# Weight tiles multiplied term by term, and a triangular inverse whose blocks VectorE turns

## The reference

```python
h = _rmsnorm(s, norm_pre_mix) * (1 + sc_a) + sh_a       # latent and context
proj = h @ w_in                                         # k, v, q, gates, z, hyena
# group A, 8 heads of 128: conv, silu, l2norm of q and k, then per chunk, both directions
a_strict   = where(strict, beta * (k k^T) * exp(diff), 0)
lower_unit = a_strict + eye
sol = triangular_solve(lower_unit, [v*beta, k*beta*exp(gcum)])
s_next = s * exp(g_last) + (k * exp(g_last - g))^T @ (u - w @ s)      # scan over the chunks
# group B: order-2 Hyena long convolution by FFT
out = concat([o, y]) @ w_out
s = s + g_a * _rmsnorm(out, norm_post_mix)
h = _rmsnorm(s, norm_pre_ffn) * (1 + sc_f) + sh_f
ff = (silu(h @ w_gate) * (h @ w_up)) @ w_down           # D_FF = 5632
s = s + g_f * _rmsnorm(ff, norm_post_ffn)
```

## Time and profile before

| | us |
|---|---|
| median of 3 runs | 1667.03 |
| the three runs | 1659.72, 1667.03, 1667.48 |
| the profiled execution | 1659.05 |
| its span | 1657.4 |
| PE busy | 1608.8 (97%), 10074 matmuls |
| DVE busy | 1148.5 (69%) |
| ACT busy | 769.1 (46%) |
| mean granted TensorE clock | 0.993 |

### The profile page before, as it was taken

How to read it: one execution, slowest core, us unless ns; L and a number is a source line. 1 busy time by engine, 2 the same in 40 slices (tenths; PEclk the granted TensorE clock), 3 DMA queues, 4 the chain that set the end, 5 groups by cost and what they waited for, 6 DMA issues and landing times.

```text
span 1657.4 us, 26938 instructions
## 1 busy us (share of the span) xinstructions
PE 1608.8 (97%) x10074; PEld 1398.9 (84%) x10074; DVE 1148.5 (69%) x1699; ACT 769.1 (46%) x1285; POOL 117.1 (7%) x214
## 2 busy tenths in 40 slices
PE   6998999999999999999998999999999999999997
PEld 2356999999998998999998888888888888888886
DVE  4726889899898997776777555555555555655665
ACT  3436465564646556433346444444444444343331
POOL 1001010110101010000110000000000000111110
PEclk9998999999999999999999999999999999999999
DMA  9996354453544545324993444554455446877872
GB/s 367 414 356 237 121 166 153 134 179 121 172 138 132 171 133 185 102 102 154 342 330 140 152 182 175 200 202 175 180 202 198 172 187 242 283 247 253 281 250 93
DMA packets 83067, 332.59 MB, mean 201 GB/s; under 512 B 8073, under 2 KB 24538, under 8 KB 56668
## 3 DMA queue, kind: packets, MB, share of 16 engines
q1 hardware_dynamic: 63168, 262.44, 43.1%
q0 software_dynamic: 19408, 67.77, 12.3%
q10 hardware_dynamic: 396, 1.10, 0.2%
HBM read 327.09 MB, written 4.19 MB: 200 GB/s over the span
## 4 chain that ended last, share of the span: by engine, by line
PE 82%; DMA 8%; DVE 5%; ACT 2%; DVEq 1%; issue 1%; SPq 0%; ACTq 0%
PE g L490 10%; PE o L490 10%; PE o L483 7%; PE o L484 7%; PE o L485 7%; PE g L491 5%; PE o L491 5%; DMA w_mod_tile_o<-in_w_mod_t 4%; DMA w_mod_raw<-in_w_mod_t 4%; PE g L566 2%; PE o L497 2%; PE g L497 2%; PE o L499 2%; PE g L499 2%; PE g L498 2%; PE g L577 2%
## 5 line engine op out<-in xcount | busy, mean ns | idle before, releaser
L464 DVE TENSOR_TENSOR w_lo<-w_raw,w_hi 128x2048 fp32r<-128x2048 f32 x202 | 462.4, 2289 | 201.8 <-ACT w_hi L459 201.4
L459 ACT CAST w_hi<-w_raw 128x2048 fp32r<-128x2048 f32 x203 | 388.0, 1911 | 219.3 <-PE o L499 73.9
L483 PE MATMUL o<-h_hi,w_hi 128*128 128x256 f32 (+1 forms) x880 | 291.6, 331 | 2.3 <-ACT hy_x L1232 1.3
L485 PE MATMUL o<-h_hi,w_lo 128*128 128x256 f32 (+1 forms) x880 | 275.3, 313 | 0.0
L484 PE MATMUL o<-h_lo,w_hi 128*128 128x256 f32 (+1 forms) x880 | 275.1, 313 | 0.0
L490 PE MATMUL g<-h_hi_lo,w_hi 128*128 128x512 f32 x704 | 245.0, 394 | 0.0
L490 PE MATMUL o<-h_hi_lo,w_hi 128*128 128x512 f32 x688 | 240.5, 394 | 2.0 <-DVE h_hi_lo L2036 2.0
L491 PE MATMUL g<-h_hi_lo,w_lo 128*128 128x256 f32 x704 | 195.0, 277 | 0.0
L491 PE MATMUL o<-h_hi_lo,w_lo 128*128 128x256 f32 x688 | 190.6, 277 | 0.0
L483 PEld LDWEIGHTS o<-h_hi,w_hi 128*128 128x128 f32 x880 | 168.0, 191 | 13.6 <-issue 6.9
L485 PEld LDWEIGHTS o<-h_hi,w_lo 128*128 128x128 f32 x880 | 167.4, 190 | 10.4
(11 more groups left out here) (393 smaller groups left out, 2820.1 us busy)
## 6 DMA issues: line engine op xcount, KB each, us to landing
w_raw<-in_w_ff_t SPq DMA_DIRECT2D x88, 1024.0 KB, 6.1
w_raw<-in_w_heads_t SPq DMA_DIRECT2D x56, 1024.0 KB, 4.9
w_mod_raw<-in_w_mod_t SPq DMA_DIRECT2D x32, 1024.0 KB, 11.1
w_raw<-in_w_down_t SPq DMA_DIRECT2D x32, 1024.0 KB, 6.8
w_mod_piece_h<-in_w_mod_t POOLq DMA_DIRECT2D x112, 256.0 KB, 3.6
w_raw<-in_w_out_t SPq DMA_DIRECT2D x16, 1024.0 KB, 8.4
w_mod_tile_o<-in_w_mod_t POOLq DMA_DIRECT2D x16, 1024.0 KB, 9.8
w_mod_piece_d<-in_w_mod_t POOLq DMA_DIRECT2D x64, 256.0 KB, 5.9
```

The lines of the kernel that those rows point to most:

```text
L459: e.copy(whi[p.split[j]][:], raw[p.raw[j]][:]).then_inc(hi_ready, 1)
L464: e.tensor_tensor(wlo[p.split[j]][:], raw[p.raw[j]][:], whi[p.split[j]][:].bitcast(F32), ALU.subtract).then_inc(lo_ready, 1)
L483: e.matmul(o, a, xh, start=first, stop=False)
L485: return e.matmul(o, b, xh, start=False, stop=last)
```

## The change

1. The three matmuls of a block no longer stand together. `mm_term` runs a tile's 16 upper x upper matmuls, then the 16 upper x lower, then the 16 lower x upper. PE waits for the upper part before the first, and for the lower part only before the last third. The FFN does its 16 matmuls of 512 columns and then its 16 of 256. Not changed are the k and v tiles of head 0, the first two tiles of the output projection, the first two of the FFN, and the down projection.
2. For the levels 2 to 5 the steps `X{n}` (ACT) and `DN{n}` (PE) are gone. DVE turns X straight from PSUM by 32x32 blocks, drains, and masks the result in place. Level 6, with blocks of 64, stays as it was.
3. The steps `v0` to `v3` move from DVE to ACT. `v0` runs at the end of the head before, the others at the end of `vs0` to `vs2`. Three drains ahead of `w{n}` on DVE go, and `w{n}` waits for ACT's `v{n}`. PE's `z0` waits for `Z` of DVE explicitly.
4. In the lists some steps change places: `D3` goes ahead of the attention masks, `D4` ahead of the convolution `cv(2)`, `D5` ahead of a piece, and a weight piece each ahead of `UT2` and `UT5`.

```diff
+        def mm_term(e, o, p, i, j, xh, xl, r0, r1, n=KT_N):
+            s = p.split[j]
+            for r in range(r0, r1):
+                term, k = r // n, r % n
+                if r == 0:
+                    upper_ready(e, p, i, j)
+                elif r == 2 * n:
+                    lower_ready(e, p, i, j)
+                last = e.matmul(o, (wlo if term == 2 else whi)[s][:, k * P:(k + 1) * P], (xl if term == 1 else xh)(k),
+                                start=(r == 0), stop=(r == 3 * n - 1))
+            return last
...
-            inv("UT1"); scan("z3"); pr(15); scan("o3"); inv("DN2"); inv("Y2"); pr(16); inv("UT2"); pr(17); pr(18); pr(19)
-            inv("DN3"); inv("Y3"); pr(20); pr(21); inv("UT3"); pr(22); pr(23); inv("DN4"); inv("Y4"); pr(24); pr(25)
+            inv("UT1"); scan("z3"); pr(15); scan("o3"); inv("Y2"); pr(16); pr(17); inv("UT2"); pr(18); pr(19)
+            inv("Y3"); pr(20); pr(21); inv("UT3"); pr(22); pr(23); inv("Y4"); pr(24); pr(25)
...
             def ff_tiles(p, i, m0, j0=0):
                 for j in range(j0, 4):
-                    tile_ready(pe, p, i, j)
                     b = (O[0], O[1], G[2], G[3])[j]
+                    pe.wait_ge(hi_ready, st.tile(p, i, j) + 1)
                     pe.wait_ge(ff_act, m0 + 2 * i + j // 2 + 1)
                     for k in range(KT_N):
-                        last = mm_pair(pe, b, p.split[j], k, h2[:, k], h2h[:, k], k == 0, k == KT_N - 1)
+                        mm_upper(pe, b, p.split[j], k, h2[:, k], k == 0)
+                    pe.wait_ge(lo_ready, st.tile(p, i, j) + 1)
+                    for k in range(KT_N):
+                        last = mm_lower(pe, b, p.split[j], k, h2h[:, k], k == KT_N - 1)
...
+            def value(d, n):
+                c = ORDER[d][n]
+                act.activation(vt[d][:, 0], vtok[u][:, c], ACT.Copy, scale=hvv[u][:, HALF_BETA, c, d:d + 1])\
+                    .then_inc(scan_act[d], 1)
...
             elif step[0] == "D" and n > 1:
-                w_ip(v, h, f"DN{n}")
-                last = v.tensor_tensor(bD[:], chunks(Z), mid(lev[:, 6 + n]), mulv)
+                v.transpose(flat(bD), X[:, :])
+                v.drain()
+                last = v.tensor_tensor(bD[:], bD[:], mid(lev[:, 6 + n]), mulv)
...
-            if step[0] == "w":
-                v.drain()
...
+                    w_sa(v, d, h, f"v{n}")
...
-                uhc2(); scan2("vs0"); ev(4); re(5); scan2("vs1"); ev(5); re(6); ev(6); scan2("vs2"); re(7); ev(7); re(8)
+                scan2("v0"); uhc2(); scan2("vs0"); ev(4); re(5); scan2("vs1"); ev(5); re(6); ev(6); scan2("vs2"); re(7); ev(7); re(8)
```

More of the change, by code:

```diff
@@ L631, in head_piece @@
             if k0 == 0:
-                tile_ready(pe, p, i, j)
                 wait_count(pe, evac, tile_number(p, i, j) - 1)
-            for k in range(k0, k1):
-                last = mm3(pe, b[:, :n], p.split[j], k, hh[:, k, :n], hl[:, k, :n], k == 0, k == KT_N - 1)
+            if p is H0 and kind in "kv":
+                if k0 == 0:
+                    tile_ready(pe, p, i, j)
+                for k in range(k0, k1):
+                    last = mm3(pe, b[:, :n], p.split[j], k, hh[:, k, :n], hl[:, k, :n], k == 0, k == KT_N - 1)
+            else:
+                last = mm_term(pe, b[:, :n], p, i, j, lambda k: hh[:, k, :n], lambda k: hl[:, k, :n], 3 * k0, 3 * k1)
             if k1 == KT_N:
@@ L801, in tail_pe @@
             inv("kk"); scan("o2"); scan("z3"); pr(8); pr(9); inv("u"); scan("o3"); pr(10); inv("Y1"); pr(11); pr(12)
-            inv("UT1"); pr(13); inv("DN2"); inv("Y2"); scan("tr"); pr(14); inv("UT2"); pr(15); inv("DN3"); inv("Y3")
-            pr(16); inv("UT3"); pr(17); inv("DN4"); inv("Y4"); pr(18); inv("UT4"); pr(19); inv("DN5"); inv("Y5"); pr(20)
+            inv("UT1"); pr(13); inv("Y2"); scan("tr"); pr(14); inv("UT2"); pr(15); inv("Y3")
+            pr(16); inv("UT3"); pr(17); inv("Y4"); pr(18); inv("UT4"); pr(19); inv("Y5"); pr(20)
             inv("UT5"); pr(21); inv("DN6"); inv("Y6"); uh2(); pr(22); inv("UT6"); pr(23); hu(0); scan2("z0"); pr(24); scan2("s0"); hu(1)
@@ L937, in out_tile @@
             def out_tile(j):
-                tile_ready(pe, W, 0, j)
                 pe.wait_ge(wo_free, j + 3)
-                for k in range(KT_N):
-                    last = mm3(pe, O[j % 2][:, :SEQ], W.split[j], k, mh[:, k], ml[:, k], k == 0, k == KT_N - 1)
-                last.then_inc(w_used, 1)
+                mm_term(pe, O[j % 2][:, :SEQ], W, 0, j, lambda k: mh[:, k], lambda k: ml[:, k], 0, 3 * KT_N).then_inc(w_used, 1)
                 sum_squares(j + 1, (j + 1) % 2, False)
@@ L1088, in scan_act_ @@
                 return
+            def value(d, n):
+                c = ORDER[d][n]
+                act.activation(vt[d][:, 0], vtok[u][:, c], ACT.Copy, scale=hvv[u][:, HALF_BETA, c, d:d + 1])\
+                    .then_inc(scan_act[d], 1)
+            if step == "v0":
+                act.drain()
+                for d in BOTH:
+                    w_sp(act, d, h - 1, "z3")
+                    value(d, 0)
+                return
             n = int(step[2])
@@ L1096, in scan_act_ @@
                     act.copy(vt[d][:, 1], F[d][:, at_chunk(0)]).then_inc(scan_act[d], 1)
+            if n < 3:
+                for d in BOTH:
+                    value(d, n + 1)
         def uh_act(act, h):
@@ L1623, in scan_dve_ @@
             n = int(step[1])
-            if step[0] == "v":
-                if n == 0:
-                    v.drain()
[L1627 to L1634, removed]
-            if step[0] == "w":
-                v.drain()
             for d in BOTH:
```

73 lines of the change are left out of this document (44 added, 29 removed).

## The result

| | before | changed |
|---|---|---|
| median of 20 runs each, us | 1666.76 | 1669.21 |
| lowest and highest | 1655.84, 1672.72 | 1666.89, 1676.04 |
| profiled execution and its span | 1659.05, 1657.4 | 1671.74, 1669.8 |

The ratio is 1.0035, 95% interval [1.002, 1.005]: slower by more than the measurement is uncertain, and within 0.5%; the two medians alone lie 0.15% apart. The time was forecast at 1666.6 us. It came close by luck, because two misses of opposite sign cancel. The heads 1 to 6 lost 10.1 us where the sum had 1.6, and the feed-forward layer won about 7 us in most runs, which the sum took for a constant.

A forecast was written before the change was run, and what follows sets the result against it. PE and DVE were both taken as full in the heads, DVE setting the period after the change. Heads 1 to 6 +1.6, head 0 +1.0, tail -2.6, output projection -0.4, order 0: -0.4 us, so 1666.6 us, range 1651 to 1681.

The forecast's parts named there:

- The price of a turn: Heads, levels 2 to 5 on DVE: a turn with its drain costs 0.76 us like a copy, +3.04 for four.
- PE's saving: Inside a head: four `DN` leave PE at 0.44 us each, 1.76 us, bringing PE's period to 68.80 us.
- DVE now sets the period: Heads 1 to 6: DVE's work 69.73 us exceeds PE's 68.80; waits on PE go; +0.26 us a head.
- a forecast 2.36: DVE in a head: removing the `v` steps and three drains ahead of `w` takes off 2.36 us.
- ACT's side: Heads: four copies of X go, eight 128x128 instructions come, nearly cancelling; nothing waits for ACT except at one tail place.
- Head 0 and tail: Head 0: between 0 and +2 us, taken as +1.0; tail after the last head's start: -2.6 us.
- The order of the matmuls: Gate and up: sorting 512- and 256-column matmuls changes -0.4 us, taken as 0, within 4 us either way.
- The median of the runs is 8.0 above it: Whole kernel: 8.0 us added to the profiled-execution forecast of 1658.7 us, giving 1666.6 on the median's scale.
- PE kept no bound alone: Faster rival, heads: PE keeps the bound, period falls toward 68.80 us, -15.3 us in all, 1651.7; chance 0.2.
- the turn did not cost two passes: Slower rival, heads 0 to 6: each turn takes 0.61 us more, +16.7 us in all, 1683.7; chance 0.17.
- the reordering does nothing: Rival on matmul order: PE did not wait for lower parts, so later waits change nothing; inside the forecast, no separate chance.
- a DVE that falls behind for another reason: Slower case: DVE falls behind through, for example, the DMA wait or new waits on ACT's values; chance 0.08.

The follow-up runs named there:

- e1: Not a run but a step of the kernel: an activation on ACT (ScalarE) in each head, for which PE waits 0.36 us in the changed kernel.

## Why the prediction was right or wrong

**The price of a turn: right.** 0.79 us measured for the 0.76 taken from the copy, and 0.79 by doubling. The Trainium skill, "Vector Engine (DVE) Microarchitecture Reference", section 3.8, has the 32x32 transpose at one element per cycle and lane, the price of a copy; the trace agrees with 0.71 us against 0.69. The Trainium skill's 311 ns for a 128x128 bf16 tile ("VectorE: DVE Perf Modes", section "The three transpose paths"), from which the prediction worked out an estimated 1.24 us a level, does not scale by four to this form, which lasts 0.71. The prediction's word that the trace disagrees with 390 ns on TensorE goes too far: its 0.11 us are a distance between starts, and one turn lasts 0.27 us (L572).

**PE's saving: right in size.** One level less takes 0.44 us off a gapless period: 70.56 to 70.12.

**The step that failed: "DVE now sets the period. Its waits on PE, 0.97, go, because PE is now the one that waits."** The sum took two engines' loads and let the larger one run without waits on the other. DVE's own work came out as forecast, about 69.7 us: 72.2 less 2.1 of waits and some 0.4 for what each costs beside its bracket. The waits on transfers came to 1.0 us a head, near the 1.09 of the sum. But the waits on PE did not go: they are 1.1 us a head (3.9 + 0.6 in four), twice the 0.5 that these four heads had before. This is nearly the whole miss, +1.6 us a head for +0.26.

Why they stayed shows in the parts. The turns, 3.04 us, all fell into the second part of DVE's head, from which only v3 and a drain, 0.55, had gone and which had 0.7 us of waits to give: it grew by 1.94. The rest of what the value steps gave back lay in the first part. There PE is busy for 19.00 us and waits 0.36 for `e1`, so DVE could not use what it had won and waited for `kk` instead (1.24 us in the head shown). A period of two nearly full engines is a sum over parts, each as long as the engine that is later in it, and not the larger of two sums.

Three runs carry this. With the turns and without the moved value steps a head takes 72.9 us, DVE full and never waiting on PE. Moving the value steps brought it to 72.3, and to 71.7 with `v2` out of the way of `e1`: 0.6 and 1.2 us for a forecast 2.36. That the turns cost in full is shown by doubling them (+3.16 for four); that fewer of them pay, by the runs with one and with two levels. The changed places in the lists (point 4 of the change) were never run alone against the old ones with four turns, so what they add or take is not known.

**ACT's side: wrong in one place.** That "nothing waits for it but at one place in the tail" missed `e1`: v1 and v2 stand ahead of it and held PE 0.36 us a head. Moving v2 alone behind it took this wait away and 0.6 us off a head.

**Head 0 and tail.** Head 0 was forecast at +1.0 and measured -1.2, but it scatters: 67.2, 66.1, 66.6 and 66.4 us in four profiles of before. The kernels with the new order and no turn in head 0 have 65.4 to 66.5, those with four turns 65.5 to 67.0. What the turns cost there is not told apart from this scatter. In the tail the four turns were worth -3.0 (forecast -1.76 and -1.4). The value steps on ScalarE gave 0.8 to 1.4 of it back (forecast 0.6): 122.3 and 122.9 us in two runs that have them, 121.5 in two that don't. The profile of after has 125.7 us, +1.5 against before, where the run without the order of terms has 122.4. The two profiles also differ in the clock: after was granted 1.2 GHz from about 657 to 664 us, and the other run 2.4 over its whole tail. Seven us at half speed are an estimated 3.5 us, about the difference. The wait of 2.9 moved from `z0` to `s0` as forecast and is 3.3 now, and the fall of the clock lies at its end. The wait, and then the busy time of a stretch behind it, with the clock at 0.50 of full:

```profile
657.96 1.22 PE L645 MATMUL g<-v_scaled,k_tok 128*128 128x128 f32 x4 [3.31 <-ACT v_scaled L1139]
```

```profile
658.00:660.00 2.00, 2.00 (x9) 2.00 (x10) 0.58 (x2) 2.00 (x8) 0.00 (x0) 0.50 1.01 410
```

**The order of the matmuls: right for the profile, wrong for the median.** A pair at 0.348 in place of 0.3467 us is the "0 within 4 us" of the sum. The failed step is "The median of the runs is 8.0 above it": the 8 us were carried over as if they belonged to the run and not to the code. They are gate and up at 0.3533 us a pair: 498.9 us for 489.7 and 490.5 in the other group, some 9 us, in three of four runs of before (15 of 20). None of the twelve profiles of the sorted order has that pace. On the median's scale it is worth 6.2 us (the order alone) to 6.7 us (the change without it), and this hid most of the heads' loss.

**The rivals.** Neither priced one came. PE kept no bound alone, and the turn did not cost two passes. The third, that the reordering does nothing, holds within 4 us for the profiled execution and not for the median. Nearest came the case that the chances had at 0.08, a DVE that falls behind for another reason; the reason was its waits for `kk`. One sentence there contradicts the sum: by the sum DVE's period passes the present one already with turns at their forecast price (70.56 + 0.26). What goes from a gain to a loss at +0.02 us a turn is the total.

## What to carry to other kernels

When two engines are both nearly full, don't compare their sums. Cut the period at the handovers between them and ask of each instruction moved in which part it lay and whether that part had a wait: work taken out beside a wait buys little (here 0.6 to 1.2 us of 2.36), work put where there is none costs in full (3.16 us for four turns). Move as little as evens the two out (here one level of four), and take the place with idle time first (here the last head).

If the timed runs fall into two groups, profile one of each before you forecast. The distance between them may be a property of the very code that is changed.

## What the runs showed of the hardware

PE alternating between matmuls of 512 and 256 columns, without a gap and at full clock, had two paces in these runs, 0.3467 and 0.3533 us a pair, 1.9% apart, each constant over the stage of 490 us. In the small group the 512-column steps of one profile go between 0.230 and 0.233 us and are 0.230 in the other; in the large one they go round in 0.236, 0.233, 0.241. What chooses between them was not found; it differs between runs of one kernel on one chip, and the group sizes differ between chips (4 of 25 runs in the small group on one, 15 of 24 on another). Sorting the matmuls by size gave one pace, 0.3480, in twelve profiles, 0.4% above the better of the two.
